# Expert loop of a hybrid decoder step: VectorE's value-tile splits ahead of the row products, and two row updates in the next turn

## The reference

```python
def block(xb):
    q = (xb @ w_q).reshape(blk, PEER_HEADS, 2, PEER_D_HALF)
    ...
    eidx = jnp.take_along_axis(cidx, ti, axis=-1)
    gates = jax.nn.softmax(tv, axis=-1)
    u = jnp.take(u_tab, eidx, axis=0)
    act = jax.nn.gelu(jnp.einsum('nd,nhkd->nhk', xb, u).astype(jnp.float32), approximate=False)
    coef = (gates * act).astype(xb.dtype)
    return jnp.einsum('nhk,nhkd->nd', coef, jnp.take(v_tab, eidx, axis=0))
```

## Time and profile before

| | us |
|---|---|
| median of 3 executions | 4740.64 |
| their lowest and highest | 4730.73, 4758.2 |
| the profiled execution's own time | 4764.74 |
| its span, first to last instruction | 4762.9 |
| its granted TensorE clock, mean | 0.972 |

### The profile page before, as it was taken

How to read it: one execution, slowest core, us unless ns; L and a number is a source line. 1 busy time by engine, 2 the same in 40 slices (tenths; PEclk the granted TensorE clock), 3 DMA queues, 4 the chain that set the end, 5 groups by cost and what they waited for, 6 DMA issues and landing times. The chain is left out here.

```text
span 4762.9 us, 76052 instructions
## 1 busy us (share of the span) xinstructions
PE 4488.8 (94%) x29021; PEld 4347.6 (91%) x29021; DVE 3088.7 (65%) x5460; ACT 1163.7 (24%) x2078; POOL 2173.6 (46%) x1486
## 2 busy tenths in 40 slices
PE   8999999999979998998999989988999999999998
PEld 6999999899858888998899979988999999999998
DVE  4224640120337674354498889978889998899998
ACT  3102320111224332013222234331222222122222
POOL 0233223223122221335055558865666666666663
PEclk9999999999989998999999999999999999999999
DMA  6122222433531112444222249999999999999997
GB/s 192 45 67 76 94 94 95 109 101 99 188 107 45 45 45 90 135 126 133 86 79 76 74 169 361 359 344 333 319 326 333 332 331 313 326 333 352 348 326 247
DMA packets 578766, 911.55 MB, mean 191 GB/s; under 512 B 150760, under 2 KB 398568, under 8 KB 578469
## 3 DMA queue, kind: packets, MB, share of 16 engines
q1 hardware_dynamic: 430240, 422.36, 27.6%
q0 software_dynamic: 111744, 406.90, 24.1%
q10 hardware_dynamic: 36640, 80.36, 4.6%
HBM read 775.67 MB, written 133.84 MB: 191 GB/s over the span
## 5 line engine op out<-in xcount | busy, mean ns | idle before, releaser
L2601 PE MATMUL ea_banks<-h_high,ea_uT_high 128*128 128x336 f32 x2048 | 658.6, 322 | 24.4 <-DVE ea_uT_low L2631 10.5
L2601 PE MATMUL ea_banks<-h_high,ea_uT_low 128*128 128x336 f32 x2048 | 654.5, 320 | 0.0
L2601 PE MATMUL ea_banks<-h_low,ea_uT_high 128*128 128x336 f32 x2048 | 650.8, 318 | 0.0
L121 PE MATMUL p_in<-h_high,w_in_high 128*128 128x352 f32 x1536 | 495.5, 323 | 0.0
L121 PE MATMUL p_in<-h_low,w_in_high 128*128 128x352 f32 x1536 | 492.3, 321 | 0.0
L121 PE MATMUL p_in<-h_high,w_in_low 128*128 128x352 f32 x1536 | 491.9, 320 | 0.0
L2576 POOL DMA_INDIRECT ea_u_raw<-in_peer_v,gt_index x192 | 294.0, 1531 | 265.0 <-DVE h_low_plain L3632 207.0
L2601 PEld LDWEIGHTS ea_banks<-h_high,ea_uT_high 128*128 128x128 f32 x2048 | 390.2, 191 | 25.6 <-issue 14.6
L2576 POOL DMA_INDIRECT yT<-in_peer_u,gt_index x256 | 330.3, 1290 | 132.4 <-issue 48.5
L2601 PEld LDWEIGHTS ea_banks<-h_low,ea_uT_high 128*128 128x128 f32 x2048 | 390.1, 190 | 0.0
L2601 PEld LDWEIGHTS ea_banks<-h_high,ea_uT_low 128*128 128x128 f32 x2048 | 389.0, 190 | 0.0
(11 more groups left out here) (528 smaller groups left out, 11692.1 us busy)
## 6 DMA issues: line engine op xcount, KB each, us to landing
w_in_raw<-in_w_in SPq DMA_DIRECT2D x88, 512.0 KB, 3.8
ex_gate<-tmp_gates SPq DMA_DIRECT2D x64, 672.0 KB
ea_u_raw<-in_peer_uT SPq DMA_DIRECT2D x66, 512.0 KB
w_mb_raw<-in_peer_v SPq DMA_DIRECT2D x64, 512.0 KB
ea_uT_low_plain<-in_peer_uT SPq DMA_DIRECT2D x62, 512.0 KB
ex_lv_low_plain<-in_peer_v SPq DMA_DIRECT2D x62, 512.0 KB
tmp_acts<-ea_coef ACTq DMA_DIRECT2D x64, 336.0 KB
tmp_gates<-yT SPq DMA_DIRECT2D x28, 768.0 KB
```

The costliest lines, as they stand in the source:

```text
L121: last = pe.matmul(banks[0:rows, n, 0:CH], a[:, kk, 0:rows], b[:, kk, chunk(n)], start=(kk == 0 and a is wt.high[s] and b is high), stop=( ...
L2601: last = pe.matmul(acts.banks[:, n, 0:CD], a[:, c, :], b[:, c, dense(n)], start=(c == 0 and a is acts.uT_high[s] and b is high), stop=(c = ...
```

## The change

VectorE's turn gets another order. `cut_v` 0 and 1 and `cut_stash` 0 and 1 come directly behind `cut_live`, with no row between them. Then come rows 18 and 19 of the turn before (`take_rows(g - 1, ROWS - 2, ROWS)`), then `cut_live_v` x2, and then rows 0 to 7 in one block. At the end of a turn rows 18 and 19 are left out, but for the last turn, which does them as before. Number and size of all instructions stay the same, and no other engine's program is touched.

```diff
                 for s in range(2):
-                    take_row(g, s)
                     cut_v(g, s)
-                take_row(g, 2)
                 for s in range(2):
                     cut_stash(g, s)
-                take_rows(g, 3, 5)
                 if not first:
+                    take_rows(g - 1, ROWS - 2, ROWS)
                     for s in range(2):
                         cut_live_v(g - 1, s)
-                take_rows(g, 5, U_ROWS)
+                take_rows(g, 0, U_ROWS)
                 if first:
                     dve.wait_ge(x2_in, 16)
                     dve.wait_ge(sums_here, G)
@@
                 if not last:
                     weigh_stash(g + 1, 1)
                 sum_up(g, 7)
-                take_rows(g, v + 10, ROWS)
+                if last:
+                    take_rows(g, v + 10, ROWS)
```

## The result

| | before | after |
|---|---|---|
| median us | 4743.91 (6 runs) | 4809.81 (6 runs) |
| lowest and highest | 4730.73, 4758.2 | 4806.32, 4815.08 |
| span of the profiled execution | 4762.9 | 4807.5 |
| turn length, from the first `cut_live` to the last, / 31 | 47.28 | 48.89 |

The ratio is 1.0154, with a 95% interval of 1.012 to 1.0188 (the quotient of the two medians, 1.0139, lies in it). The medians are 66 us apart, against 48 us forecast, and the time is inside the range that was stated.

What follows compares the result with a forecast made beforehand. VectorE's own chain of work and waits was taken to close each turn. Row and gate waits rising from 3.35 to 4.9 us a turn, x 31, added 48 us to the 4740.64 us median: 4789 us, range 4690 to 4845.

Steps and rivals of the forecast that it cites:

- What bounds: In the expert loop, VectorE's work (43.13 us a turn) plus its row and gate waits closes the 47.28 us turn.
- (a): The live value cut ends 6.0 us earlier, so TensorE's wait for it goes; by itself this brings nothing.
- (b): The stash cut ends 5.8 us earlier and the gates' load follows it; the 1.4 us gate wait a turn goes.
- (c): Rows 18 and 19, holding the buffers of rows 3 and 4, are used 5.3 us later, delaying gathers 3 to 7.
- R: VectorE's waits for gathered rows in a turn after the change, taken as 4.9 us, between 1.6 and 7.3.
- four counts: Row waits a turn by row 3's gather length and transfer time: 5.2 or 4.1 us short, 7.3 or 5.2 long.
- short gather: Row 3's gather let in at the first border between two VectorE instructions: 1.74 us, in 7 of 29 turns.
- The long count: Gather 3 ends at 4037.8, after row 0; row waits 7.3 us a turn, or 5.2 with 4.5 us transfers.
- long gather: Row 3's gather held past three borders up to row 0's accumulator read: 4.41 us, in 21 turns before.
- the fourth rival: Row 3's gather is long in every turn with today's transfer times: row waits 6.2 to 7.3, 4829 to 4863 us; chance 0.15.
- The sum: Row and gate waits go from 3.35 to 4.9 us a turn: +1.55, x 31 = +48 us, giving 4789 us.
- The small waits: VectorE's other idle time in a turn: some 1.2 us in one place, 0.8 us, unchanged, in the forecast's total.

Runs made afterwards that it cites:

- `after_gaps`: The changed kernel plus three one-column VectorE memsets, behind rows 18 and 19 and behind each live value cut; ratio to before 1.0078.
- `cuts_first`: The kernel before with only VectorE's cuts brought together at the head of the turn, rows 18 and 19 left in their own turn; ratio 1.0151.
- `rows_moved_only`: The kernel before with only rows 18 and 19 moved, behind the next turn's live cuts; value and stash cuts stay between rows; ratio 1.0120.
- `before_wait_row19`: The kernel before with VectorE waiting, ahead of the first live cut, until its own row 19 is finished; ratio 0.9944.

## Why the prediction was right, point by point

- What bounds: right. VectorE's work was 43.4 us a turn (43.13 before) and the time followed its waits.
- (a) The live value cut: right. TensorE's wait for it is gone, and the kernel is slower all the same; no run took away this wait alone. Its new wait is at a bank addition, as was said.
- (b) The gates: right. No wait for them is left.
- (c) The size: right, in part by luck. R was set at 4.9 us; the row waits are 148.4 / 31 = 4.8 us, and "about 150 us" was the mark set for the profile. The loop grew by 49.9 us between the two profiled executions, against 48 forecast. But 4.9 was a middle between four counts, two of them with the short gather, which hardly ever came. Where it did come in every turn, in `after_gaps`, the row waits were 114.2 / 31 = 3.7 us and not the 4.1 or 5.2 counted.
- (c) The cause: half wrong. The prediction put the loss down to the two rows that hold buffers 3 and 4, "5.3 us later". `cuts_first` leaves them in place and loses the same 1.5%. With the cuts in front, the lateness came from the block of cuts, which held no opening for GpSimd until row 0's accumulator read. The buffers' share shows where something else doesn't hide it: with openings (1.0078 against 1.0021), and with the cuts in their old places (`rows_moved_only`, 1.0120). The long count did have this border in it: its 4.41 us row reached to the accumulator read, and the same rule gave 4037.8 us for the end of gather 3, which is 12.1 us behind the last bank addition. The trace after has 4047.60 - 4035.55 = 12.05. So the prediction priced this border, but did not name it as the cause.
- Chance of the long gather: too low. It stood in the fourth rival at 0.15, with the transfer times of now. In fact 30 of 31 turns had it; only the transfers were shorter, as rows 3 to 5 of the turn shown started 4.3, 4.2 and 5.0 us behind their gathers, so that R was 4.8 and not 7.3. Long gather and 4.5 us transfers was one of the four counts, at 5.2.
- The sum: by medians the loss is 66 us and not 48. The term that was mis-sized is the base: the profiled execution of before lay 21 us above the median, and the sum took its 47.28 us turns as typical. The kernel before has two kinds of turn (48.07 and 45.62 us), so a run's time may hang on how many of each it has. Its six runs beside the changed kernel spread by 0.6% (4731 to 4758 us) and those of the changed kernel by 0.2%. That the share of short turns makes this spread was not measured.
- Two smaller slips. The small waits are 1.2 us a turn in one place and 0.8 in the sum, where they are called unchanged; with 1.2 the forecast would have been 4801 us. The whole waits table gives them about 0.9 before and 0.7 after. And of the 14.3 us between rows 1 and 7, 4.9 us are other work (one value cut, the stash cuts and the live value cuts in the earlier trace rows) and not 6.9; no sum used this.
- The rule of the Trainium skill that was weighed, page "SBUF — State Buffer", section "SBUF: two separate sides", an exclusive lock held for one instruction: the gathers that end 0.94 us behind a border (1.74 us in `after_gaps`) agree with it, but the hold of up to 9.5 us in `cuts_first`, over nine borders, is longer than one instruction. The measurement decides.

## What to carry to other kernels

When GpSimd makes gathers beside VectorE, look at the length of each gather in the timeline: one that is longer than the shortest was held up, and its end less the shortest length tells which VectorE instruction let it in. When you reorder VectorE, keep an opening (in this kernel an accumulator read, an instruction that reads PSUM, a one-column memset or a short idle) behind each instruction that frees a gather's buffer. Don't expect anything from taking a wait off TensorE when another engine closes the turn. And test a cause and its size apart: here the number came out while the cause was half wrong.

## What the runs showed of the hardware

- A gather's descriptors (0.94 us of GpSimd) can be held up for 9.5 us by an unbroken run of VectorE instructions with two SBUF inputs (10.49 us in `cuts_first`, 29 of 31 turns).
- A memset of one column between two such instructions admitted gather 3 in every one of 31 turns and costs next to nothing: from one live value cut to the next it is 1.15 us with a memset between them (4024.59 - 4023.44 in `after_gaps`), and 1.14 without. One such line in the kernel before makes it 0.7% faster (0.9931). An idle time of VectorE of 0.13 us did the same (`before_wait_row19`).
- Accumulator reads and bank additions, which read PSUM, were never passed by: in the trace before, 105 of 105 gathers that waited when a row's accumulator read came were let in there, and 107 of 107 that waited when a bank addition followed a row.
- Without an opening, the same border between the same two instructions (row 19 and the first live cut) lets GpSimd in in some turns (1.74 us) and not in others (4.41 us). In the trace before these turns last 45.6 and 48.1 us on the mean, and the first kind are those in which VectorE had waited for TensorE ahead of its last bank addition.
- Where VectorE waited for a gathered row (128 rows of 4 KB), its work on it began 3.3 to 8.1 us behind the end of the descriptors, in the traces before and after, while the DMA engines were 0.92 to 0.95 busy.
